# Where the mixer's result is transposed ahead of the out-projection in a two-layer decoder kernel

## The chip, the cores and the metric

The kernel runs on one core of one Trainium2 chip. The metric is the device time of one execution in microseconds; for several runs it is their median. A core has TensorE (PE in the profile; PEld is its weight load), VectorE (DVE), ScalarE (ACT), GpSimd (POOL) and SyncE (SP), which here only issues transfers.

## What is computed

Two layers over 256 tokens of width 1024, all in float32. Layer 0 mixes by retention and HGRN2, layer 1 by stick-breaking and differential attention; each has one combined input projection and one output projection. After each mixer stands a mixture of experts with 32 experts, of which each token uses two.

```python
for l in range(DEPTH):
    h = rms_norm(x, norm_mix[l])
    if l % 2 == 0:
        mix = retention_hgrn2_mixer(h, w_in_ab[j], w_out_ab[j], ...)
    else:
        mix = stickbreak_diff_mixer(h, w_in_cd[j], w_out_cd[j], ...)
    x = x + mix
    h = rms_norm(x, norm_ffn[l])
    x = x + hierarchical_moe(h, ..., w_gate[l], w_up[l], w_down[l])

# the end of either mixer; layer 0 as an example
    ret = rms_norm(ret, ret_gain).reshape(B, S, RET_WIDTH) * jax.nn.silu(rg)
    o = rms_norm(o, hgrn_gain).reshape(B, S, ...) * jax.nn.silu(hg)
    mixed = jnp.concatenate([ret, o], axis=-1)      # (1, 256, 1024)
    return mixed @ w_out                            # w_out: (1024, 1024)
```

## The kernel before

Every weight is used once and comes from HBM in units of 2048 KB. The SP queue issues them in one fixed order (`load_unit`, its transfer at L328) into eleven places: six in `ring`, five in `wide`. A place that was in use is waited for through the semaphore `unit_used`, which TensorE raises when it has done the last matmul on a unit. Per layer the order is: the blocks of the input projection (8 in layer 0, 6 in layer 1), the two halves of w_out (places 2 and 3), then 96 expert units. Expert units 0 to 3 use places 4, 5, 0, 1; then the queue waits until both halves of the mixer's result are gated (`gated`), issues units 4 to 7 into places 6 to 9 of `wide`, and units 8 and 9 into places 2 and 3, which the two halves of w_out must have left. Unit 10 waits for the router's logits (L796) and unit 11 for place 4, which the first expert matmuls free.

Each engine runs its own hand-written order of work. The part around the change:

- `project(layer, n)` multiplies the normalized tokens `hT` by block n (L741): 16 products of 128x128 by 128x512, each two records in the trace (x32), two token blocks (`tc`) of eight products. Results go to PSUM banks 0, 1 or 2, 3 in turn (`proj(g)`). Its argument `meanwhile` is a list of functions that are called after each quarter of the block. The last block of layer 0 is `project(0, 7)`, to banks 2 and 3. ACT takes its sigmoid (L1074), VectorE multiplies twice (L1409, and `gate_it` at L1424), and with that the second half of `mixed` is gated. The first half of `mixed` (retention) is gated by the same line one block earlier.
- `mixed` holds tokens on the partitions, so TensorE must transpose it before the out-projection: `turn_mixed(pe, half)` (L707), eight 128x128 transposes for each half into banks 0 and 1. The halves use the same banks. `keep_mixT` (L712) copies a turned half from PSUM to `hT`: the first half by ACT in `finish_mixer`, the second by VectorE in its own `finish_mixer`.
- `project_out(layer)` (L783) is, for each half: wait until it is gated, transpose it, wait for the copy, and do 16 products on it with that half of w_out, accumulating in banks 4 to 7, token block by token block. VectorE then adds to `x` (L1199).
- `route_and_experts` follows: x is transposed (L697, copied at L701), the router's logits are made (L796), VectorE selects (L1245 to L1292) and builds one-hot matrices (L596), TensorE gathers the tokens of four experts at a time (L475), and the expert matmuls run (L519) for eight quads of four experts. In quad 0 and in the last matrix the weights come in quarters over all four experts, and each quarter frees its unit by itself.
- In layer 1 the first half of `mixed` (stick-breaking) is gated by a copy at L1547 and the second at L1555, behind an inverse root that ACT and VectorE do together (`take_root`).
- `y_sb` is a buffer of 128x1024 that only the expert stage uses; it is cleared at L584 ahead of it.

Of the kernel before, what the change touches and what calls it, by code (L numbers as in the profile page):

```python
# [23 lines left out]
P = 128  # L24
SEQ = 256
# [100 lines left out]
def build(nc, t, where, const_width, stop_after=4):  # L126
    with ExitStack() as ctx:
        def sb(name, shape, dt=F32):
            return ctx.enter_context(nc.sbuf_tensor(name, shape, dt))

        def sem(name):
            return ctx.enter_context(nc.semaphore(name))
# [11 lines left out]
        psum = ctx.enter_context(nc.psum_tensor("psum", [P, 8, 512], F32))  # L144
# [4 lines left out]
        def part(who, width, shape=None, **dims):  # L149
            a = taken.get(who, 0)  # L150
            taken[who] = a + width
            assert taken[who] <= (arena_w, UNIT)[who == "last"], (who, taken)
            a += arena_w * (who == "last")
            v = wide[:, a:a + width]
            return v.rearrange(shape, **dims) if shape else v

        hT = part("last", KC * SEQ, "p (c t) -> p c t", c=KC)
# [48 lines left out]
        y_sb = sb("y_sb", [P, D])[:, :]  # L206
# [30 lines left out]
        S = {n: sem(n) for n in names}  # L237
        proj_used = [sem(f"proj_used{i}") for i in range(2)]
# [15 lines left out]
        def unit_base(layer):  # L254

            return layer * (UNITS_IN[0] + UNITS_OUT + n_moe)
# [28 lines left out]
        def slot(layer, n):  # L285

            place = unit_place(layer, n)
            return ring[:, place, :] if place < RING else wide[:, (place - RING) * UNIT:(place - RING + 1) * UNIT]
# [5 lines left out]
        def wait_unit(eng, layer, n):  # L294
            eng.wait_ge(unit_landed[unit_place(layer, n)], unit_landings(layer, n))
# [6 lines left out]
        def proj(g):  # L302

            return psum[:, 2 * (g % 2):2 * (g % 2) + 2, :]

        def wait_projected(eng, n):

            eng.wait_ge(S["unit_used"], n if n <= UNITS_IN[0] else unit_base(1) + n - UNITS_IN[0])

        def flat(a):  # L310
            return a.rearrange("p a b -> p (a b)")
# [336 lines left out]
        def take_root(act, turn):  # L648
            col, count = ROOTS[len(roots_taken)]
            roots_taken.append(col)  # L650
            act.wait_ge(S["root_in"], len(roots_taken))
            y = small[:, 64:64 + count]
            turn(nc.scalar.activation(y, small[:, col:col + count], ACT.Ln))
            nc.scalar.activation(y, y, ACT.Exp, scale=-0.5).then_inc(S["root_out"], 1)
# [48 lines left out]
        def turn_mixed(pe, half):  # L703

            for tc in range(TC):
                for c in range(4):
                    mm = pe.transpose(psum[:, c // 2, (c % 2) * SEQ + tc * P:(c % 2) * SEQ + (tc + 1) * P],  # L707
                                      mixed[:, tc, (4 * half + c) * P:(4 * half + c + 1) * P], ident)
            mm.then_inc(S["mix_turned"], 1)

        def keep_mixT(half, copy):
            return copy(hT[:, 4 * half:4 * half + 4, :].rearrange("p (b c) t -> p b (c t)", b=2), psum[:, 0:2, :])  # L712

        def keep_hT(half, copy):
            return copy(hT[:, 4 * half:4 * half + 4, :].rearrange("p (b c) t -> p b (c t)", b=2),  # L715
# [6 lines left out]
        def _(pe):  # L722
            def project(layer, n, meanwhile=()):


                g = (0, UNITS_IN[0])[layer] + n
                wait_unit(pe, layer, n)
                if g >= 2:

                    pe.wait_ge(proj_used[g % 2], g // 2)  # L730
                w = slot(layer, n).rearrange("p (c n) -> p c n", c=KC)
                banks = proj(g)
                if BLOCKS[layer][n] in TURNED[layer]:
                    for m in range(HEADS):
                        for c in range(KC):
                            mm = pe.matmul(banks[:, m // 2, (m % 2) * SEQ:(m % 2 + 1) * SEQ],  # L736
                                           w[:, c, m * P:(m + 1) * P], hT[:, c, :], start=c == 0, stop=c == KC - 1)
                else:
                    for tc in range(TC):
                        for c in range(KC):  # L740
                            mm = pe.matmul(banks[:, tc, :], hT[:, c, tc * P:(tc + 1) * P], w[:, c, :],  # L741
                                           start=c == 0, stop=c == KC - 1)
                            quarter = (tc * KC + c + 1) // (KC // 2)
                            if (c + 1) % (KC // 2) == 0 and quarter <= len(meanwhile):
                                meanwhile[quarter - 1]()
                mm.then_inc(S["unit_used"], 1)
# [6 lines left out]
            def attend(bank, hd, s, v):  # L753

                cols = slice(hd * HD, (hd + 1) * HD)
                pe.matmul(psum[:, bank, cols], s[:, 0:P], v[:, 0, cols], start=True, stop=True)
                pe.matmul(psum[:, bank + 1, cols], s[:, P:SEQ], v[:, 0, cols], start=True, stop=False)
                mm = pe.matmul(psum[:, bank + 1, cols], s[:, SEQ:TRI], v[:, 1, cols], start=False, stop=True)
                mm.then_inc(S["pv_done"], 1)

            def turn_roped(col):
# [4 lines left out]
                                          mixed[:, tc, col + hd * HD:col + (hd + 1) * HD], ident)  # L766
                mm.then_inc(S["turned"], 1)

            def project_out(layer):

                for half in range(2):

                    pe.wait_ge(S["gated"], 2 * layer + half + 1)
                    if half == 0:
                        pe.wait_ge(proj_used[0], (4, 7)[layer])
                    turn_mixed(pe, half)
                    pe.wait_ge(S["mixT_ready"], 2 * layer + half + 1)
                    wait_unit(pe, layer, UNITS_IN[layer] + half)
                    w = slot(layer, UNITS_IN[layer] + half).rearrange("p (c n) -> p c n", c=4)
                    for tc in range(TC):  # L780
                        for c in range(4):
                            for n in range(2):
                                mm = pe.matmul(psum[:, 4 + 2 * tc + n, :], hT[:, 4 * half + c, tc * P:(tc + 1) * P],  # L783
                                               w[:, c, 512 * n:512 * (n + 1)], start=half == 0 and c == 0,
                                               stop=half == 1 and c == 3)
                        if half == 1 and tc == 0:
                            mm.then_inc(S["out_first"], 1)
                    mm.then_inc(S["unit_used"], 1)
# [81 lines left out]
            pe.wait_ge(S["st_ready"], 2 * HEADS)  # L870
            for hd in range(HEADS):
                attend(4, hd, st2[:, hd, :], val2)
            project(0, 7)

            pe.wait_ge(S["out_used"], 2)
            project_out(0)
# [33 lines left out]
            def diff_turn(hd):  # L910

                pe.wait_ge(S["diff_a"], hd + 1)
                if hd >= 2:
                    pe.wait_ge(S["diff_aT"], hd - 1)
                a = dff[:, hd % 2, :]
                pe.transpose(psum[:, hd % 2, 0:P], a[:, 0:P], ident)
                pe.transpose(psum[:, hd % 2, P:SEQ], a[:, P:SEQ], ident)
                pe.transpose(psum[:, hd % 2, SEQ:TRI], a[:, SEQ:TRI], ident).then_inc(S["diff_turned"], 1)
# [30 lines left out]
            def diff_attend(hd):  # L949
                pe.wait_ge(S["diff_aT"], hd + 1)  # L950
                attend(2, hd, st[:, hd % 2, :], val2)
# [9 lines left out]
            for hd in range(2, HEADS):  # L961
                diff_turn(hd)
                diff_attend(hd)
            project_out(1)
            route_and_experts(1)

# [4 lines left out]
        def _(act):  # L971
# [14 lines left out]
                act.wait_ge(S["h_turned"], n // 2 + 1)  # L986
                keep_hT(0, nc.scalar.copy).then_inc(S["hT_ready"], 1)

            def finish_mixer(layer):

                act.wait_ge(S["mix_turned"], 2 * layer + 1)
                keep_mixT(0, nc.scalar.copy).then_inc(S["mixT_ready"], 1)
                nc.scalar.preload_act_table_set(LOG_EXP)
                square(act, 2 * layer + 1, 0)
                act.wait_ge(S["x_turned"], TC * layer + 1)
                keep_xT(0, nc.scalar.copy).then_inc(S["xT_first"], 1)
                square(act, 2 * layer + 1, 1)
                take_root(act, turn)
# [71 lines left out]
            act.wait_ge(S["pv_done"], 2 * HEADS)  # L1070
            nc.scalar.activation(tmp, flat(psum[:, 4:6, :]), ACT.Square).then_inc(S["sq_out"], 1)
            take_root(act, turn)
            wait_projected(act, 8)
            nc.scalar.activation(flat(qT), flat(proj(7)), ACT.Sigmoid).then_inc(S["gate_sig"], 1)  # L1074
            finish_mixer(0)
# [76 lines left out]
            act.wait_ge(S["pv_done"], 4 * HEADS)  # L1152
            nc.scalar.activation(tmp1, flat(psum[:, 2:4, :]), ACT.Square).then_inc(S["sq_out"], 1)
            take_root(act, turn)
            finish_mixer(1)
            route(1)
            moe_act(act, 1, 0, 0)
# [429 lines left out]
```

## Time and profile before

| what | value |
|---|---|
| median of 3 runs | 1288.95 us (1288.56 to 1290.48) |
| profiled execution | 1287.09 us |
| its span in the trace | 1285.1 us |
| PE busy | 993.1 us (77%) |
| VectorE busy | 243.0 us (19%) |
| ScalarE busy | 153.8 us (12%) |
| moved by DMA | 448.53 MB, mean 349 GB/s |
| L519, expert matmuls | 406.5 + 401.4 us |
| L741, in-projections, 128x512 | 145.5 us |
| L783, out-projections | 58.7 us |

The profile is one execution. Its own time is 2.0 us over its span. PE busy is no measure of load, since TensorE also shows as busy while it works at a lower clock; the granted clock stands in a row of its own. A chain of waits follows the execution back from its last instruction, at each step to what released it. Times are from the span's start; layer 0's mixer lasts to about 206 us, its experts to about 660, layer 1's mixer to about 826.

### The profile page before, as it was taken

Reading aid. Unit: us, or ns where it says so; the run is one execution under the profiler, and the core shown is the slowest. Engines: PE = TensorE matmul, PEld = TensorE weight load, DVE = VectorE, ACT = ScalarE, POOL = GpSimd, SP = SyncE. Lnnn points to the kernel's source line nnn. Section 1 sums busy time; section 2 is a strip of 40 time slices with the busy share of each in tenths; the row PEclk is TensorE's granted clock in tenths of the full one; section 3 lists DMA queues with packets and bytes.
Section 4 is the critical chain, followed back from the end, with each engine's and each line's share of the span. In section 5 each row is a group of like instructions: output and inputs, shape, how many; then the busy total and the mean of one; then the engine's idle time right before and its main releaser. Section 6 shows DMA issues by size and latency. Waiting matters only on the chain.

```text
span 1285.1 us, 12164 instructions
## 1 busy us (share of the span) xinstructions
PE 993.1 (77%) x5148; PEld 433.0 (34%) x5148; DVE 243.0 (19%) x668; ACT 153.8 (12%) x320; POOL 12.6 (1%) x12
## 2 busy tenths in 40 slices
PE   5999998986767776766759987997776867767765
PEld 5657645421212121212227544542212312121211
DVE  3410225111101000101030564331101101000101
ACT  3523311100000000000021222110000000000000
POOL 0000001000000000000000000100000000000000
PEclk9988899987879878878789998998877878778878
DMA  7963067899999999999997413869999999999995
GB/s 248 302 248 131 14 279 296 341 429 427 428 429 426 429 426 429 427 428 428 417 392 255 149 69 148 340 280 430 427 428 427 428 427 428 427 429 426 429 421 218
DMA packets 62150, 448.53 MB, mean 349 GB/s; under 512 B 13072, under 2 KB 13328, under 8 KB 39568
## 3 DMA queue, kind: packets, MB, share of 16 engines
q1 hardware_dynamic: 62096, 447.73, 84.5%
q8 instruction: 44, 0.72, 0.2%
q14 instruction: 10, 0.08, 0.0%
HBM read 446.66 MB, written 1.05 MB: 348 GB/s over the span
## 4 chain that ended last, share of the span: by engine, by line
DMA 48%; PE 42%; SPq 4%; DVE 3%; ACT 1%; issue 1%; DVEq 0%; ACTq 0%
PE psum L519 17%; DMA ring<-in_w_up 14%; PE psum L741 11%; DMA ring<-in_w_down 10%; DMA wide<-in_w_gate 10%; DMA wide<-in_w_down 9%; DMA ring<-in_w_gate 5%; PE psum L783 5%; PE psum L736 2%; SPq L384 2%; SPq L328 1%; PE psum L475 1%; PE psum L836 1%; PE psum L482 1%; PE psum L838 1%
## 5 line engine op out<-in xcount | busy, mean ns | idle before, releaser
L519 PE MATMUL psum<-ring,mixed 128*32 128x512 f32 x1664 | 406.5, 714 | 123.8 <-DMA ring<-in_w_up 54.2
L519 PE MATMUL psum<-wide,mixed 128*32 128x512 f32 x1408 | 401.4, 710 | 108.8 <-DMA wide<-in_w_gate 62.4
L519 PEld LDWEIGHTS psum<-ring,mixed 128*32 128x32 f32 x1664 | 93.0, 128 | 328.1 <-issue 162.0
L519 PEld LDWEIGHTS psum<-wide,mixed 128*32 128x32 f32 x1408 | 88.6, 127 | 274.1 <-issue 123.2
L741 PE MATMUL psum<-ring,wide 128*128 128x512 f32 x320 | 145.5, 613 | 0.6 <-DMA ring<-in_w_in_ab 0.6
L741 PEld LDWEIGHTS psum<-ring,wide 128*128 128x128 f32 x320 | 62.3, 198 | 76.9 <-issue 75.8
L623 DVE TENSOR_TENSOR mixed<-psum,sig 128x512 f32<-128x512 f32 x16 | 16.9, 1056 | 277.9 <-PE psum L519 277.9
L482 PE MATMUL psum<-y_sb,spread 128*128 128x512 f32 x144 | 66.6, 605 | 1.6 <-DVE y_sb L628 1.6
L475 PE MATMUL psum<-sel,h 128*128 128x128 f32 x520 | 64.4, 283 | 3.5 <-DVE sel L596 3.5
L475 PEld LDWEIGHTS psum<-sel,h 128*128 128x128 f32 x520 | 61.0, 196 | 17.1 <-issue 13.4
L783 PE MATMUL psum<-ring,wide 128*128 128x512 f32 x128 | 58.7, 618 | 6.1 <-ACT wide L712 3.5
L567 ACT COPY mixed<-psum 128x1024 f32<-128x1024 f32 x18 | 18.2, 1012 | 355.1 <-PE psum L475 355.1
L736 PE MATMUL psum<-wide,ring 128*128 128x256 f32 x256 | 57.3, 387 | 2.7 <-DVE wide L715 2.7
L620 DVE TENSOR_TENSOR sig<-psum,sig 128x512 f32<-128x512 f32 x16 | 11.1, 692 | 240.8 <-ACT sig L573 240.8
L736 PEld LDWEIGHTS psum<-wide,ring 128*128 128x128 f32 x256 | 49.5, 194 | 10.3 <-DVE wide L715 3.4
L628 DVE COPY y_sb<-psum 128x512 f32<-128x512 f32 x16 | 11.1, 692 | 194.0 <-PE psum L519 194.0
L604 DVE TENSOR_SCALAR selw<-consts,rank,wtab 128x32 f32<-128x32 f32 x144 | 31.4, 296 | 50.6 <-PE psum L548 50.5
L573 ACT ACTIVATE sig<-psum 128x512 f32<-128x512 f32 x16 | 9.6, 597 | 257.2 <-PE psum L519 257.2
L482 PEld LDWEIGHTS psum<-y_sb,spread 128*128 128x128 f32 x144 | 25.9, 189 | 42.7 <-issue 39.2
L783 PEld LDWEIGHTS psum<-ring,wide 128*128 128x128 f32 x128 | 25.0, 198 | 37.6 <-issue 30.4
L580 ACT COPY y_sb<-psum 128x512 f32<-128x512 f32 x16 | 9.4, 586 | 206.1 <-PE psum L519 206.1
L596 DVE TENSOR_SCALAR sel<-consts,rank,small 128x32 f32<-128x32 f32 x144 | 31.4, 295 | 1.6 <-PE psum L475 1.5
(238 smaller groups left out, 529.9 us busy)
## 6 DMA issues: line engine op xcount, KB each, us to landing
ring<-in_w_down SPq DMA_DIRECT2D x38, 2048.0 KB, 35.1
ring<-in_w_up SPq DMA_DIRECT2D x36, 2048.0 KB, 37.7
wide<-in_w_gate SPq DMA_DIRECT2D x34, 2048.0 KB, 36.6
ring<-in_w_gate SPq DMA_DIRECT2D x30, 2048.0 KB, 30.9
wide<-in_w_up SPq DMA_DIRECT2D x28, 2048.0 KB, 28.5
wide<-in_w_down SPq DMA_DIRECT2D x26, 2048.0 KB, 34.7
ring<-in_w_in_ab SPq DMA_DIRECT2D x8, 2048.0 KB, 16.6
ring<-in_w_in_cd SPq DMA_DIRECT2D x6, 2048.0 KB, 21.4
```

Of the source, the lines that this page charges most:

```text
L328: sp.dma_start(dst_cols(slot(layer, n)), src).then_inc(unit_landed[unit_place(layer, n)], 16)
L384: sp.dma_start(dst, src).then_inc(S["small_landed"], 16)
L475: mm = pe.matmul(psum[:, YB + c // 4, (c % 4) * P:(c % 4 + 1) * P], h[:, tc, c, :], sel[:, tc, :], start=tc == 0, stop=tc == TC - 1)
L482: mm = pe.matmul(psum[:, ACC + 2 * tc + n, :], spread[:, tc, :], y_sb[:, 512 * n:512 * (n + 1)], start=False, stop=False, skip_group_check ...
L519: mm = pe.matmul(psum[slots, out + n, :], inp[:, c, slots], slot(layer, unit)[:, at + 512 * n:at + 512 * (n + 1)], start=c == 0, stop=c == ...
L567: nc.scalar.copy(xT, psum[:, YB:YB + 2, :].rearrange("p b (c s) -> p (b c) s", s=P)).then_inc(m["xT_ready"], 1)
L596: r = nc.vector.tensor_scalar(sel[:, tc, e * SLOTS:(e + 1) * SLOTS], const("iota"), rank[:, tc, bass.ds(quad * TILE + e, 1)], small[:, 2 + ...
L604: r = nc.vector.tensor_scalar(selw[:, tc, e * SLOTS:(e + 1) * SLOTS], const("iota"), rank[:, tc, bass.ds(quad * TILE + e, 1)], wtab[:, tc, ...
L623: nc.vector.tensor_tensor(act_h.rearrange("p c s -> p s c"), psum[:, UP, :].rearrange("p (s c) -> p s c", c=FC), sig.rearrange("p (s c) -> ...
L736: mm = pe.matmul(banks[:, m // 2, (m % 2) * SEQ:(m % 2 + 1) * SEQ], w[:, c, m * P:(m + 1) * P], hT[:, c, :], start=c == 0, stop=c == KC - 1)
L741: mm = pe.matmul(banks[:, tc, :], hT[:, c, tc * P:(tc + 1) * P], w[:, c, :], start=c == 0, stop=c == KC - 1)
L783: mm = pe.matmul(psum[:, 4 + 2 * tc + n, :], hT[:, 4 * half + c, tc * P:(tc + 1) * P], w[:, c, 512 * n:512 * (n + 1)], start=half == 0 and ...
```

## The change

The second half of `mixed` is transposed into banks 2 and 3 in place of 0 and 1, and this is done in both layers between the first and the second token block of the first half's out-projection (`turn_half(layer, 1)`). The first half is transposed before `project_out`: in layer 0 inside the last in-projection, between its two token blocks, in layer 1 where it was. The first half's copy goes to `y_sb` in place of `hT`; on ACT it is a function of its own, `keep_first_half`, which stands in layer 0 ahead of the last gate's sigmoid. The waits for the gate and for the bank go with the transposes.

```diff
@@ -704,12 +704,16 @@
 
             for tc in range(TC):
                 for c in range(4):
-                    mm = pe.transpose(psum[:, c // 2, (c % 2) * SEQ + tc * P:(c % 2) * SEQ + (tc + 1) * P],
+                    mm = pe.transpose(psum[:, 2 * half + c // 2, (c % 2) * SEQ + tc * P:(c % 2) * SEQ + (tc + 1) * P],
                                       mixed[:, tc, (4 * half + c) * P:(4 * half + c + 1) * P], ident)
             mm.then_inc(S["mix_turned"], 1)
 
+        def mixT(half):
+
+            return hT[:, 4:8, :] if half else y_sb.rearrange("p (c t) -> p c t", c=4)
+
         def keep_mixT(half, copy):
-            return copy(hT[:, 4 * half:4 * half + 4, :].rearrange("p (b c) t -> p b (c t)", b=2), psum[:, 0:2, :])
+            return copy(mixT(half).rearrange("p (b c) t -> p b (c t)", b=2), psum[:, 2 * half:2 * half + 2, :])
 
         def keep_hT(half, copy):
             return copy(hT[:, 4 * half:4 * half + 4, :].rearrange("p (b c) t -> p b (c t)", b=2),
@@ -766,23 +770,26 @@
                                           mixed[:, tc, col + hd * HD:col + (hd + 1) * HD], ident)
                 mm.then_inc(S["turned"], 1)
 
+            def turn_half(layer, half):
+
+                pe.wait_ge(S["gated"], 2 * layer + half + 1)
+                pe.wait_ge(proj_used[half], (4, 7)[layer])
+                turn_mixed(pe, half)
+
             def project_out(layer):
 
                 for half in range(2):
-
-                    pe.wait_ge(S["gated"], 2 * layer + half + 1)
-                    if half == 0:
-                        pe.wait_ge(proj_used[0], (4, 7)[layer])
-                    turn_mixed(pe, half)
                     pe.wait_ge(S["mixT_ready"], 2 * layer + half + 1)
                     wait_unit(pe, layer, UNITS_IN[layer] + half)
                     w = slot(layer, UNITS_IN[layer] + half).rearrange("p (c n) -> p c n", c=4)
                     for tc in range(TC):
                         for c in range(4):
                             for n in range(2):
-                                mm = pe.matmul(psum[:, 4 + 2 * tc + n, :], hT[:, 4 * half + c, tc * P:(tc + 1) * P],
+                                mm = pe.matmul(psum[:, 4 + 2 * tc + n, :], mixT(half)[:, c, tc * P:(tc + 1) * P],
                                                w[:, c, 512 * n:512 * (n + 1)], start=half == 0 and c == 0,
                                                stop=half == 1 and c == 3)
+                        if half == 0 and tc == 0:
+                            turn_half(layer, 1)
                         if half == 1 and tc == 0:
                             mm.then_inc(S["out_first"], 1)
                     mm.then_inc(S["unit_used"], 1)
@@ -870,7 +877,7 @@
             pe.wait_ge(S["st_ready"], 2 * HEADS)
             for hd in range(HEADS):
                 attend(4, hd, st2[:, hd, :], val2)
-            project(0, 7)
+            project(0, 7, (lambda: None, lambda: turn_half(0, 0)))
 
             pe.wait_ge(S["out_used"], 2)
             project_out(0)
@@ -961,6 +968,7 @@
             for hd in range(2, HEADS):
                 diff_turn(hd)
                 diff_attend(hd)
+            turn_half(1, 0)
             project_out(1)
             route_and_experts(1)
 
@@ -986,10 +994,13 @@
                 act.wait_ge(S["h_turned"], n // 2 + 1)
                 keep_hT(0, nc.scalar.copy).then_inc(S["hT_ready"], 1)
 
-            def finish_mixer(layer):
+            def keep_first_half(layer):
 
                 act.wait_ge(S["mix_turned"], 2 * layer + 1)
                 keep_mixT(0, nc.scalar.copy).then_inc(S["mixT_ready"], 1)
+
+            def finish_mixer(layer):
+
                 nc.scalar.preload_act_table_set(LOG_EXP)
                 square(act, 2 * layer + 1, 0)
                 act.wait_ge(S["x_turned"], TC * layer + 1)
@@ -1070,6 +1081,7 @@
             act.wait_ge(S["pv_done"], 2 * HEADS)
             nc.scalar.activation(tmp, flat(psum[:, 4:6, :]), ACT.Square).then_inc(S["sq_out"], 1)
             take_root(act, turn)
+            keep_first_half(0)
             wait_projected(act, 8)
             nc.scalar.activation(flat(qT), flat(proj(7)), ACT.Sigmoid).then_inc(S["gate_sig"], 1)
             finish_mixer(0)
@@ -1152,6 +1164,7 @@
             act.wait_ge(S["pv_done"], 4 * HEADS)
             nc.scalar.activation(tmp1, flat(psum[:, 2:4, :]), ACT.Square).then_inc(S["sq_out"], 1)
             take_root(act, turn)
+            keep_first_half(1)
             finish_mixer(1)
             route(1)
             moe_act(act, 1, 0, 0)
```

## Rows read from the trace of the kernel before

**Rows 1.** The page, part 4: shares of the chain that ended last, by engine.

```profile
DMA 48%; PE 42%; SPq 4%; DVE 3%; ACT 1%; issue 1%; DVEq 0%; ACTq 0%
```

**Rows 2.** Stretches: length, busy time of five engines, granted clock, DMA share, GB/s.

```profile
217.00:221.00 4.00, 1.08 (x8) 0.97 (x8) 3.29 (x17) 1.49 (x2) 0.00 (x0) 1.00 0.44 188
221.00:225.00 4.00, 3.75 (x19) 3.75 (x20) 3.65 (x20) 0.00 (x0) 0.00 (x0) 0.57 0.00 0
840.00:845.00 5.00, 3.84 (x32) 3.65 (x32) 4.65 (x25) 0.69 (x1) 0.00 (x0) 1.00 0.00 0
...
231.00:620.00 389.00, 282.05 (x1700) 91.78 (x1692) 40.94 (x133) 20.72 (x35) 0.00 (x0) 0.84 1.01 427
849.00:1235.00 386.00, 278.19 (x1668) 90.81 (x1662) 40.85 (x133) 20.72 (x35) 0.00 (x0) 0.84 1.01 427
```

**Rows 3.** Timeline of the SP queue, issues of weight units: start, us, instruction.

```profile
177.80 1.76 SPq L328 DMA_DIRECT2D wide<-in_w_up  x4
...
229.81 0.33 SPq L328 DMA_DIRECT2D ring<-in_w_down  x1
231.53 3.76 SPq L328 DMA_DIRECT2D ring<-in_w_gate  x3
245.56 0.33 SPq L328 DMA_DIRECT2D wide<-in_w_gate  x1
...
847.39 0.33 SPq L328 DMA_DIRECT2D ring<-in_w_down  x1
```

**Rows 4.** Chain of waits, layer 0: start us, us, what.

```profile
160.39 13.75 PE psum L741 x32
174.16 1.02 ACT wide L1074
...
176.14 14.00 PE psum L783 x32
190.14 0.89 PE psum L707 x8
...
191.06 1.24 DVE wide L712
...
192.33 14.01 PE psum L783 x32
...
221.25 5.44 PE psum L475 x32
```

**Rows 5.** Chain of waits, layer 1.

```profile
792.64 16.68 PE psum L783 x32
809.32 0.89 PE psum L707 x8
810.23 1.24 DVE wide L712
811.51 14.02 PE psum L783 x32
...
840.43 3.84 PE psum L475 x32
```

**Rows 6.** Chain at 733.86 us; stretches there and before layer 1's out-projection.

```profile
733.86 0.87 PE psum L765 x8
...
733.00:735.00 2.00, 2.00 (x15) 1.71 (x15) 1.55 (x3) 1.10 (x2) 0.00 (x0) 1.00 0.77 174
...
788.00:798.00 10.00, 7.68 (x18) 4.18 (x18) 4.75 (x10) 3.62 (x5) 0.00 (x0) 0.50 0.19 52
```

**Rows 7.** Timeline of VectorE and ScalarE: gates of the halves, a table load.

```profile
160.13 1.22 DVE L1424 TENSOR_TENSOR mixed<-mixed,wide 128x1024 f32<-128x1024 f32 x1
...
163.41 1.28 ACT L1074 ACT_TABLE_LOAD   x1
...
176.55 1.23 DVE L1424 TENSOR_TENSOR mixed<-mixed,wide 128x1024 f32<-128x1024 f32 x1
...
793.99 1.29 DVE L1555 TENSOR_TENSOR mixed<-mixed,subln 128x512 f32<-128x512 f32 x2
```

## The prediction

> **What bounds the kernel now.** I read the chain of waits first. It is split almost evenly between waiting for DMA (48%) and TensorE work (42%) [rows 1]. A share over the whole span does not say which microseconds count, so the next question is where the DMA stream is unbroken. The table by stretch shows it: from 231 to 620 us and from 849 to 1235 us the DMA engines are busy all the time at 427 GB/s, while in 221 to 225 and in 840 to 845 us they move nothing [rows 2]. So each layer has two regimes: a mixer that TensorE and its waits pace, then an expert stage that the DMA paces. What ties them is the SP queue [rows 3]: after a gap an expert unit is issued at 229.81 in layer 0 and at 847.39 in layer 1, and the unbroken stream begins with it. Both issues wait for a ring place that the first expert matmuls (gate projection, quad 0) free. The stream then takes a fixed time, so an earlier start of the expert matmuls moves the end of the layer one for one. The chain through the mixer is therefore worth its full length.
>
> In that chain [rows 4], layer 0: last in-projection 160.39 to 174.16; ACT's sigmoid (1.02), then ACT's copy of the first turned half; first half of the out-projection 176.14 to 190.14; eight transposes (0.89); VectorE's copy of the second half (1.24); second half from 192.33. The first eight transposes lie beside the sigmoid. In layer 1 [rows 5]: 792.64 the first half, 809.32 transposes (0.89), 810.23 the copy (1.24), 811.51 the second half. While these copies run, TensorE has nothing.
>
> **The change part by part.**
>
> *Second half turned amid the first half's out-projection, both layers.* The eight transposes do not vanish: they stand after the first eight products of the half and cost 0.89 there as before. What goes is the wait for the copy: layer 0, 192.33 - (190.14 + 0.89) = 1.30; layer 1, 811.51 - (809.32 + 0.89) = 1.30 [rows 4, 5]. The copy now lies beside the remaining token block, half of 14.00 = 7.0 us, against its 1.24; that is the cover, 5.8 to spare. It can do so since the second half goes to banks 2 and 3, and the two halves' results no longer share banks.
>
> *First half turned amid the last in-projection, layer 0.* ACT copies it behind the sigmoid, from 174.16 + 1.02 = 175.18 to about 176.14 (so 0.96), and only then the out-projection starts [rows 4]. After the change the transposes stand near 160.39 + 13.75/2 = 167.3 and ACT copies to y_sb by about 169.2, with 5.8 us to spare. The in-projection ends later by the transposes. Their price bounded from both sides: 0.87 (eight transposes between two projections) [rows 6] and 0.89 [rows 4]; I take 0.88. The out-projection starts at 174.16 + 0.88 = 175.04 instead of 176.14: a gain of 1.10. In layer 1 the first half is turned and copied where it was, in the same order on ACT, so nothing is gained there.
>
> *Waits that are added or move.* Inside the in-projection TensorE now waits for the first half's gate. That gate, queued on VectorE, ends at 160.13 + 1.22 = 161.35 [rows 7], 5.9 us before TensorE comes by. Queued behind this wait is the second token block of the projection; it is not touched. Inside the out-projection TensorE waits for the second gate. In layer 0 this gate ends today at 176.55 + 1.23 = 177.78 [rows 7]; sigmoid and gate follow the end of the in-projection, so it moves to 178.66, and TensorE comes by at 175.04 + 7.0 = 182.04: 3.4 to spare. In layer 1 it ends at 793.99 + 1.29 = 795.28 [rows 7], and TensorE comes by about 7.0 before 809.32, at 802.3. ACT's copy now stands ahead of the sigmoid in ACT's queue; the sigmoid's table load (1.28) [rows 7] may slip behind the copy, to about 170.5, still ahead of 175.04. None costs anything while these margins hold; if the second gate were 4 us later, TensorE would wait for the rest.
>
> *The SP queue.* It waits for the second gate too, so in layer 0 its four units at 177.80 go out 0.88 later. A unit of 2048 KB takes about 4.9 us at 427 GB/s, and the unit before it is freed by the in-projection's end, at 175.04; so the engines still have work until about 180. The unit that the first half of w_out frees goes out with the end of that half, today 176.14 + 14.00 = 190.14, then 175.04 + 14.00 + 0.88 = 189.92; the two behind it, for the second half and the logits, about 2.4 earlier. After the restart four units are on the way (229.81 and three from 231.53), 19.7 us of transfer, and the next release comes at 245.56, 15.8 after 229.81 [rows 3]: the stream has no hole, and these releases move with TensorE.
>
> *Sum.* Layer 0: 1.10 + 1.30 = 2.40. Layer 1: 1.30. Together 3.70. The profiled execution took 1287.09 us (span 1285.1 and 2.0 around it): 1287.09 - 3.70 = 1283.4. The median of the runs is 1288.95, so by the same sum **1285.2 us**.
>
> *What the trace leaves uncertain: the clock.* The 32 gather matmuls took 5.44 in layer 0 [rows 4] and 3.84 in layer 1 [rows 5]; in the first the granted clock was at 1.2 GHz for part of the time (0.57 on the mean in 221 to 225), in the second at 2.4 GHz (1.00 in 840 to 845) [rows 2]. Ahead of the slow one TensorE was busy for 1.08 of 4 us, in 217 to 221 [rows 2]. So the chain of a layer varies by 1.60 with where the fall lies, and a shift of the work by 2.4 us can move it either way: both gathers slow, or both fast. This gives 1285.2 + 1.6 = 1286.8 and 1285.2 - 1.6 = 1283.6. The Trainium skill (TensorE: Matmul & The Clock Gate, What's actually happening) says that the same kernel shows a differing number of slow matmuls from run to run, since the monitor is not aligned with its start; no single trace can show that.
>
> **The rivals.** By 0.2% (2.6 us) I mean about what a measurement of this kernel can tell from no change.
>
> *Rival 1, the clock draw takes the gain:* both gathers in the slow clock, 1286.8, 0.17% faster and so no measurable change. For it: one of two did so before. Against: equally likely the other way.
>
> *Rival 2, the stream holds the end:* the DMA share of 48% is what counts, and an earlier mixer only lengthens a wait. 1288.95. Against it: nothing moves in 221 to 225, and the releases at 229.81 and 847.39 are TensorE's.
>
> *Rival 3, the early turn in layer 0 does not do what it says:* the wait inside the in-projection or ACT's queue gives back the 1.10, and the layer 0 copy gives only part: 1.3 to 2.6 in all, 1286.9 at 2.1. Against: margins of 3.4 to 5.9.
>
> *Rival 4, slower:* transposes amid matmuls pull the clock down. A low stretch of TensorE with small work ahead of it cost much in layer 1: 788 to 798 ran at 0.50 [rows 6], and that out-projection half took 16.68 [rows 5] where its twin took 14.00 [rows 4], 2.68 more. If each of the three insertion places brought one such stretch: 3 x 2.68 - 3.70 = +4.3, 1293.3. It decides from two such stretches on (5.4 against 3.7); over 0.2% needs three. Against: eight transposes between two projections stand at 733.86, and the clock in 733 to 735 is 1.00 [rows 6], with dense matmuls on both sides, just as in the new places. The Trainium skill (TensorE: Matmul & The Clock Gate, Part 4: PE-mode transpose) states the rule behind this rival: transposes do not count as busy like matmuls do, and the full clock does not engage for them. By that rule short insertions might lower the clock; the trace disagrees at the one place that resembles the new ones.
>
> **How the numbers follow.** Forecast, 1285.2 with the gathers mixed as before: 0.60, faster. Both gathers fast, 1283.6: 0.11, faster. Rival 1: 0.14, the same. Rival 2: 0.06, the same. Rival 3: 0.05, the same. Rival 4: 0.04, slower. In the runs of before the highest lies 1.5 over the median; a repeated median of either kernel may move by about 1, which adds little on the slower side beyond rival 4. Faster 0.71, same 0.25, slower 0.04. The range takes in 1283.6 less 0.8 and 1286.8 plus 1.5: 1282.8 to 1288.3; rival 4 and most of rival 2 are left out.
>
> **What would show it.** In the changed kernel's chain: the copies at the two turns are gone from it, and each second half of the out-projection follows the first within 0.1 us; the first half in layer 0 starts within 0.1 of the in-projection's end; both halves with transposes last 14.9 (17.6 in layer 1 if the clock is again low). The copy of the first half on ACT stands near 168 to 169. The restart of the SP queue moves from 229.81 to about 227.4, give or take 1.6 with the clock, and that of layer 1 comes 3.7 earlier. The prediction is wrong if TensorE shows a wait for a gate inside either projection, if the clock is 0.50 behind an insertion, or if the time from restart to end grows.

## The result and the profile after

The changed kernel took 1282.45 us (median of 5 runs, 1280.83 to 1283.33), the kernel before 1288.95 (5 runs, 1288.35 to 1290.48). The ratio is 0.9946, with a 95% interval of 0.9931 to 0.9960: faster by 6.5 us, where 3.7 were forecast, and the time lies 0.35 below the range. All runs of both kernels together, told below, put the gain at 4.5 us. So there are two things to explain, 0.8 us that the sum lacked and 2 us that the first comparison showed too much.

The page of the changed kernel; its shares cannot be told from those of before [rows 1]:

```profile
span 1280.5 us, 12166 instructions
...
PE 993.7 (78%) x5148; PEld 434.5 (34%) x5148; DVE 243.0 (19%) x668; ACT 153.9 (12%) x320; POOL 12.6 (1%) x12
...
DMA 48%; PE 42%; SPq 4%; DVE 3%; ACT 1%; issue 1%; DVEq 0%; ACTq 0%
```

The chain of waits in layer 0 (start us, us, what), the answer to [rows 4]:

```profile
160.19 6.87 PE psum L745 x16
167.06 0.87 PE psum L707 x8
167.93 6.87 PE psum L745 x16
174.80 6.87 PE psum L788 x16
181.67 0.87 PE psum L707 x8
182.54 20.62 PE psum L788 x48
...
218.06 3.84 PE psum L475 x32
```

Line 745 is the in-projection, 707 the transposes, 788 the out-projection. The chain no longer leaves TensorE between 160.19 and 203.16. From the start of the last in-projection to VectorE's add of the second token block it is 203.18 - 160.19 = 42.99; before it was 206.37 - 160.39 = 45.98, the add's start being 192.33 + 14.01 and an issue of 0.03 behind it [rows 4]. That is 2.99 saved, where the sum had 2.40. The transposes cost 0.87 at both places, as forecast. The half with its transposes takes 6.87 + 0.87 + 6.87 = 14.61, and not the 14.9 that I wrote.

Layer 1, the answer to [rows 5]:

```profile
788.10 9.95 PE psum L788 x16
798.05 0.87 PE psum L707 x8
798.92 20.62 PE psum L788 x48
...
834.44 5.46 PE psum L475 x32
```

The SP queue (issues of weight units), the answer to [rows 3]:

```profile
178.47 1.76 SPq L328 DMA_DIRECT2D wide<-in_w_up  x4
...
225.02 0.33 SPq L328 DMA_DIRECT2D ring<-in_w_down  x1
...
843.03 0.33 SPq L328 DMA_DIRECT2D ring<-in_w_down  x1
```

The restart of the stream moved from 229.81 to 225.02 in layer 0, 4.8 earlier and 0.8 below the forecast's lower bound (227.4 - 1.6 = 225.8). 3.2 of it are the mixer's (0.2 of them lie before the last in-projection), and 1.6 are the gather: it took 3.84 here against 5.44 [rows 4]. In layer 1 it is the other way round, 5.46 against 3.84 [rows 5]. So the clock's part cancels in this pair of profiles. The expert stages keep their pace, 428 GB/s below against 427 [rows 2]. The two profiled executions, 1287.09 and 1282.45, thus differ by 4.6 us, and not by 6.5: 3.2 in layer 0's mixer and 1.45 in layer 1's, where the way from the start of the out-projection to the add went from 825.55 - 792.64 = 32.91 [rows 5] to 819.56 - 788.10 = 31.46. The slow records at its start are not at the same clock in the two; at an equal clock layer 1 is compared below.

The covers and margins of the prediction, on the timelines of ScalarE and VectorE:

```profile
167.97 1.01 ACT L716 COPY y_sb<-psum 128x1024 f32<-128x1024 f32 x1 [4.78 <-PE psum L707]
169.00 1.28 ACT L1086 ACT_TABLE_LOAD   x1
...
177.22 1.23 DVE L1437 TENSOR_TENSOR mixed<-mixed,wide 128x1024 f32<-128x1024 f32 x1
182.58 1.22 DVE L716 COPY wide<-psum 128x1024 f32<-128x1024 f32 x1 [4.13 <-PE psum L707]
```

The first half's copy stands at 167.97 (forecast 168 to 169), and the table load did slip behind it, to 169.00, done 4.5 us before the in-projection ends and the sigmoid can start. The second gate ends at 178.45 and TensorE comes by at 181.67, 3.2 later (forecast 3.4). The second copy, 182.58 to 183.80, lies beside matmuls until 189.4.

Stretches (length, busy time of five engines, granted clock, DMA share, GB/s) around the two insertions of layer 0 and of the stream:

```profile
160.00:174.00 14.00, 14.00 (x41) 6.75 (x40) 5.67 (x9) 3.73 (x5) 0.00 (x0) 1.00 0.32 130
174.00:190.00 16.00, 16.00 (x44) 7.48 (x43) 3.67 (x3) 2.31 (x2) 0.00 (x0) 1.00 0.90 363
...
230.00:620.00 390.00, 283.76 (x1676) 93.49 (x1673) 41.65 (x134) 21.32 (x36) 0.00 (x0) 0.83 1.01 428
```

The granted clock is 1.00, that is 2.4 GHz, across both insertions; the third, in layer 1, has 1.00 as well (798 to 799).

### The profile page after: what moved, and what is told of

The parts are those of the page before. It is cut to its first block, busy times and chain, and to the rows that moved or that the text cites. A ratio compares the mean times of both kernels' runs of the same rounds, so it can differ in the third digit from the quotient of the medians.

```text
span 1280.5 us, 12166 instructions
## 1 busy us (share of the span) xinstructions
PE 993.7 (78%) x5148; PEld 434.5 (34%) x5148; DVE 243.0 (19%) x668; ACT 153.9 (12%) x320; POOL 12.6 (1%) x12
## 4 chain that ended last, share of the span: by engine, by line
DMA 48%; PE 42%; SPq 4%; DVE 3%; ACT 1%; issue 1%; DVEq 0%; ACTq 0%
PE psum L519 17%; DMA ring<-in_w_up 14%; PE psum L745 11%; DMA ring<-in_w_down 10%; DMA wide<-in_w_gate 10%; DMA wide<-in_w_down 9%; DMA ring<-in_w_gate 5%; PE psum L788 5%; PE psum L740 2%; SPq L384 2%; SPq L328 1%; PE psum L475 1%; PE psum L843 1%; PE psum L482 1%; PE psum L845 1%
## 5 line engine op out<-in xcount | busy, mean ns | idle before, releaser
L519 PE MATMUL psum<-ring,mixed 128*32 128x512 f32 x1664 | 411.8, 722 | 124.4 <-DMA ring<-in_w_up 52.1
L745 PE MATMUL psum<-ring,wide 128*128 128x512 f32 x320 | 145.5, 612 | 1.9 <-DMA ring<-in_w_in_ab 1.9
L745 PEld LDWEIGHTS psum<-ring,wide 128*128 128x128 f32 x320 | 62.2, 198 | 77.5 <-issue 75.2
L788 PE MATMUL psum<-ring,y_sb 128*128 128x512 f32 x64 | 31.0, 642 | 2.3 <-ACT y_sb L716 2.3
L788 PE MATMUL psum<-ring,wide 128*128 128x512 f32 x64 | 27.8, 592 | 0.0
```

Source lines behind the costliest of these rows:

```text
L519: mm = pe.matmul(psum[slots, out + n, :], inp[:, c, slots], slot(layer, unit)[:, at + 512 * n:at + 512 * (n + 1)], start=c == 0, stop=c == ...
L788: mm = pe.matmul(psum[:, 4 + 2 * tc + n, :], mixT(half)[:, c, tc * P:(tc + 1) * P], w[:, c, 512 * n:512 * (n + 1)], start=half == 0 and c ...
```

## Experiments

The theories, made after the result above was seen. **A**: the change is worth the waits that it removes, 3.7 us, and at each of the three also a restart of TensorE, 0.26 us (work behind a wait takes that much longer than the same work behind running work), which the sum lacked; 4.5 in all, and the rest of the 6.5 is scatter. **B**: the waits had a further cost; in part of the executions the clock fell in them, which made a slow tail in the kernel before. **C**, the rival from the prediction, that the DMA stream holds the end, was tried at a larger size as well.

### The parts alone, and both kernels again

The kernel before, unchanged:

> The kernel before, unchanged, once more. Theory A (the profiled execution of before was a lucky draw, and the change is worth its removed waits plus a TensorE restart of 0.26 us each): ratio 1.000, times between 1287 and 1291 as before, and its trace has no low clock at the two copies of the turned halves (174 to 176 and 190 to 193 us). Theory B (the idle ends at these copies let the clock fall in part of the executions of before, and this is the rest of the gain): a trace of before shows a granted clock below 1.00 in 176 to 206 us, and more time there.

Measured: 1287.66 us median, ratio 1.0006 (0.9991 to 1.0020). The kernel before beside it, 35 runs on the same chip, had a median of 1287.48, a mean of 1288.0 and a range of 1284.98 to 1292.44. So the three runs of the prediction, median 1288.95, lay high, and one run scatters by more than 2 us. In its trace the clock is 1.00 all the way from 160 to 206, and the halves of the out-projection take 14.00 and 14.02: no fall at the copies, as theory A expected.

The whole change:

> The whole change, once more. Theory A: 3.7 us of removed waits plus three restarts of 0.26 us, so 4.5 us faster, ratio 0.9965. Theory B: 6.5 us faster, ratio 0.995.

Measured: 1283.56 us, ratio 0.9967 (0.9956 to 0.9978), theory A's number. Theory B's 0.995 lies outside the interval.

The second half alone:

> Only the second half is turned amid the first half's out-projection, in both layers; the first half of layer 0 is turned behind the in-projection as before. Theory A: two waits of 1.30 and two restarts of 0.26, so 3.1 us faster, ratio 0.9976. Theory B: more than that, about 4.5, since two idle stretches are gone.

```diff
-            project(0, 7, (lambda: None, lambda: turn_half(0, 0)))
+            project(0, 7)
+            turn_half(0, 0)
...
-            keep_first_half(0)
             wait_projected(act, 8)
             nc.scalar.activation(flat(qT), flat(proj(7)), ACT.Sigmoid).then_inc(S["gate_sig"], 1)
+            keep_first_half(0)
```

Measured: 1284.55 us, ratio 0.9966 (0.9950 to 0.9982). That is theory B's number (4.5 us), though the interval holds theory A's 0.9976 too. The stretch of the trace is sharper and speaks for A: layer 0 from the last in-projection's start to the add takes 203.37 - 158.96 = 44.41, 1.57 less than the 45.98 of before, against 1.56 by theory A.

The first half alone:

> Only the first half of layer 0 is turned amid the last in-projection; the second halves are turned between the two halves of the out-projection as before, though into banks 2 and 3. Theory A: 1.10 and one restart of 0.26, so 1.4 us faster, ratio 0.9989. Theory B: about 2, ratio 0.9984.

```diff
                 for half in range(2):
+                    if half == 1:
+                        turn_half(layer, 1)
                     pe.wait_ge(S["mixT_ready"], 2 * layer + half + 1)
...
-                        if half == 0 and tc == 0:
-                            turn_half(layer, 1)
```

Measured: 1286.45 us, ratio 0.9984 (0.9973 to 0.9995), which does not tell the theories apart. The same stretch of its trace takes 205.67 - 161.09 = 44.58, 1.40 less than before; theory A said 1.36. Its chain shows the restart itself, since here one half of the out-projection follows the in-projection at once and the other follows a copy:

```profile
175.70 13.73 PE psum L790 x32
189.44 0.89 PE psum L707 x8
190.35 1.24 DVE wide L716
191.63 14.02 PE psum L790 x32
```

The same 32 records take 13.73 in the first case and 14.02 in the second. The transposes behind an unbroken stream, followed by a wait, are billed 0.89, not 0.87. A stop costs its wait and also some 0.26 to 0.29 us. What TensorE does in them no row shows; I call it the restart.

### The waits filled, the wait put back

If the clock fell in the waits of the kernel before, keeping TensorE busy in them should help:

> The kernel before with two extra matmuls (128x128 by 128x256 of the constant tables, results unused) on TensorE while it waits for a copy: behind the turn of the first half in layer 0 and behind the turn of the second half in both layers. The waits stay, TensorE is not idle in them. Theory A (only the removed waits and the restarts count, and the slow tail of before, 10 of 35 executions over 1290 us, has nothing to do with these places): median as before within 0.5 us, same tail over 1290. Theory B (in part of the executions the clock falls in these waits, which makes the tail, and none of 17 executions of the changed kernel has one): the tail is gone, the mean 0.5 to 1 us lower.

```diff
+            def fill(bank, n):
+                for _ in range(n):
+                    pe.matmul(psum[:, bank, 0:SEQ], ident, ones, start=True, stop=True, skip_group_check=True)
...
                     turn_mixed(pe, half)
+                    if half == 1:
+                        fill(2, 2)
+                    elif layer == 0:
+                        fill(4, 2)
```

Measured: 1287.96 us median, 1284.98 to 1293.41, ratio 1.0003 (0.9985 to 1.0020); 4 of 12 executions lie over 1290. The tail is still there, and the mean, 1288.7, is not lower. The profiled execution was one of the tail, 1290.58 us, and it too has the clock at 1.00 from 160 to 206 and the halves at 14.00 and 14.02. Theory B falls. The chain shows where this execution lost time:

```profile
221.42 3.84 PE psum L475 x32
...
651.26 3.37 PE psum L519 x16
...
673.73 30.00 PE psum L736 x128
...
794.74 17.04 PE psum L791 x32
...
1272.36 3.43 PE psum L519 x16
```

The same places in the repeated kernel before, which took 1287.31:

```profile
221.41 5.47 PE psum L475 x32
...
652.86 1.97 PE psum L519 x16
...
673.78 27.91 PE psum L736 x128
...
792.96 16.72 PE psum L783 x32
...
1270.48 1.97 PE psum L519 x16
```

The last 16 expert records of a layer (line 519), behind the last wait for weights, take 1.97 in one and 3.37 and 3.43 in the other; the gather (line 475) takes 5.47 in one and 3.84 in the other. These are the same instructions at the two levels of the clock: its mean over the last 16 is 0.58 and 0.57 in the slow case and 1.00 in the other. The out-projection of layer 1 (line 783, 791 with the added lines) is slow in both, a little more in the first. The first 128 in-projection records of layer 1 (line 736) take 30.00 and 27.91. All these rows together make 3.6 us, and the two executions differ by 3.3. Slow last records of layer 0 come with slow first in-projection records: 3.31 to 3.37 with 29.97 to 30.00 in four traces (this one, the changed kernel's second and third repeat, and the one with a delay in the mixers, all below), 1.97 with 27.91 in the other ten, so this one draw is worth 3.4 us. All of it but the out-projection lies outside of what the change touches.

The wait for the second copy, put back into the changed kernel:

> The changed kernel, but TensorE waits for the copy of the second half directly behind its transposes, ahead of the second token block of the first half. This gives back the wait for the copy in both layers and nothing else. Theory A: 2 x (1.30 + 0.26) = 3.1 us slower than the changed kernel, 1.4 us faster than before, ratio 0.9989; the restart shows as 0.26 us on the matmuls behind the wait. Theory B: in addition some executions with a slow tail, over 1289 us.

```diff
                         if half == 0 and tc == 0:
                             turn_half(layer, 1)
+                            pe.wait_ge(S["mixT_ready"], 2 * layer + 2)
```

Measured: 1286.45 us, 1282.91 to 1288.42, ratio 0.9982 (0.9966 to 0.9998). Expected was 0.9989. The changed kernel beside it:

> The changed kernel a third time, beside the others. Theory A: 4.5 us faster than before (ratio 0.9965), 3.1 faster than the kernel with the wait put back. Theory B: 5.5 to 6.5 us faster on the mean, since before has the tail and this has not.

Measured: 1284.76 us, 1279.57 to 1286.71, ratio 0.9975 (0.9960 to 0.9990), a gain of 3.6 us by the means where theory A has 4.5. The difference of the two, 1.7 by the medians and 1.9 by the means, is short of 3.1, but each mean of 12 runs has a standard error of 0.5 to 0.6, so the times neither confirm 3.1 nor rule it out. In the traces the clock can be held equal. In layer 1 the first 16 records took 9.75 both here and in the kernel with the second half alone. With the wait:

```profile
793.41 9.75 PE psum L788 x16
803.16 0.89 PE psum L707 x8
804.08 1.24 DVE wide L716
805.36 20.88 PE psum L788 x48
826.26 1.23 DVE x L1213
```

Without it:

```profile
790.35 9.75 PE psum L788 x16
800.09 0.87 PE psum L707 x8
800.97 20.62 PE psum L788 x48
821.61 1.23 DVE x L1213
```

826.26 - 793.41 = 32.85 against 821.61 - 790.35 = 31.26, a difference of 1.59 where theory A has 1.56. In layer 0 the stretch is 205.92 - 161.35 = 44.57 with the wait and 42.99 without, 1.58.

### A known delay in either stage

> The changed kernel with 20 unused matmuls (128x128 by 128x256, 0.43 us each at full clock, 8.6 us together) on TensorE ahead of the out-projection of each layer. If the mixer's chain passes one for one to the end: 8.6 in layer 0, in layer 1 8.6 less the 2.3 in which TensorE waits there anyway, 6.3; together 14.9 us slower than the changed kernel, ratio to before about 1.008. If the DMA stream holds the end, well under half of it.

```diff
+            fill(4, 20)
             project_out(0)
...
             turn_half(1, 0)
+            fill(4, 20)
             project_out(1)
```

> The changed kernel with the same 20 unused matmuls in the expert stage instead, ahead of the third matrix of quad 3 in each layer, where TensorE waits some 31 us per quad for weights. If the stream sets the end from its restart on: 0 us, ratio to before as the changed kernel, 0.9965. If TensorE's work counts there: 17 us slower.

```diff
                 pe.wait_ge(m["xT_ready"], n17 + i + 2)
+                if not over and i == 3:
+                    for _ in range(20):
+                        pe.matmul(psum[:, YB, 0:SEQ], ident, ones, start=True, stop=True, skip_group_check=True)
                 matrix(i, 2, YB, actT, FC, D)
```

In the mixers: 1297.70 us, ratio 1.0069 (1.0048 to 1.0091), mean of 5 runs 1297.4, against the changed kernel's 1283.6 (below) 13.8 us, uncertain by 2 to 3. In the expert stage: 1283.70, ratio 0.9972 (0.9955 to 0.9989), mean of 10 runs 1283.9, 0.3 us. The same work costs most of its length in one stage and nothing that can be seen in the other. The chain with the delay in the mixers:

```profile
174.81 8.63 PE psum L781 x40
...
799.87 9.51 PE psum L781 x40
809.38 6.87 PE psum L792 x16
```

In layer 1 the filling (line 781) takes the low clock upon itself, 9.51 instead of 8.63, and the 16 out-projection records behind it run in 6.87 instead of 9.95. From the last attention records to the end of these 16 it is 816.24 - 797.26 = 18.98 here and 798.05 - 782.95 = 15.10 in the changed kernel. So layer 1 costs 3.9 (6.3 expected), and both layers 12.5 where 14.9 were expected; the measured 13.8 decides for neither. (The profiled execution itself, 1300.09, has both gathers at 5.47 and the last expert records of layer 0 at 3.31.) With the delay in the experts:

```profile
405.36 8.90 PE psum L554 x40
414.26 7.01 PE psum L519 x64
421.28 28.31 DMA ring<-in_w_up
```

The 8.90 us of filling (line 554) stand in front of a wait for weights. It begins later than in the changed kernel, 421.28 against 418.96, and ends where that one ends, 449.59 against 449.70. The stream did not change. The other traces say the same of the whole stage: from the first expert matmul to the start of the last 16 records it takes 424.4 to 425.0 us in layer 0 and 424.3 to 424.8 in layer 1 in all 14 traces, whether layer 0's begins at 221.3, as in the second repeat of the changed kernel, or at 234.4, as with the delay in the mixers. So rival 2 of the prediction is refuted, and what it was made of, a stream that cannot be hurried, is right for the other stage.

### Filling the waits where the clock does fall

> The changed kernel with unused matmuls (128x128 by 128x256) in TensorE's waits at other places: 3 and 4 of them while the router selects, in both layers, and 11 between the last attention steps of layer 1 and its out-projection. If the low clock comes from these idle stretches: both gathers at 3.8 us in place of one at 5.4, and the first 16 out-projection records of layer 1 at 7.1 in place of 9.8; 1.6 + 2.7 = 4.3 us faster than the changed kernel, and less scatter. If the clock falls all the same, the same time as the changed kernel within 1 us.

```diff
                 start_sums(pe, layer, 0)
+                fill(7, 3)
...
+                fill(7, 4)
                 moe_pe(pe, layer, 0, 0)
...
                 diff_turn(hd)
+                fill(6, 1)
                 diff_attend(hd)
+                if hd == 2:
+                    fill(6, 3)
             turn_half(1, 0)
+            fill(6, 6)
```

> The changed kernel with the 11 unused matmuls between the last attention steps of layer 1 and its out-projection alone, none in the router. The first 16 out-projection records of layer 1 at 7.1 us in place of 9.8 in each execution: 2.7 us faster than the changed kernel on the mean. If what is won there is lost later to another fall of the clock, less.

```diff
                 diff_turn(hd)
+                fill(6, 1)
                 diff_attend(hd)
+                if hd == 2:
+                    fill(6, 3)
             turn_half(1, 0)
+            fill(6, 6)
```

> The changed kernel once more, beside the others. Theory A (removed waits 3.7 plus three restarts of 0.26): 4.5 us faster than before on the mean of many executions. Theory B (a further systematic gain from the clock): 5.5 or more.

Measured, all places filled: 1283.48 us, 1278.10 to 1287.48, ratio 0.9971 (0.9955 to 0.9987), no gain over the changed kernel to be seen. Only the places ahead of the out-projection of layer 1: **1280.37 us**, 6 runs from 1279.45 to 1282.16, ratio 0.9945 (0.9926 to 0.9963). The changed kernel beside it: 1284.94, ratio 0.9965 (0.9948 to 0.9981). The version with 11 unused matmuls is the fastest of all; its mean of six, 1280.5, is 3.1 us under the changed kernel's 1283.6 (uncertain by about 1). Its chain and a stretch of its clock, then the chain of the changed kernel beside it, and the same stretch of the clock in the changed kernel's first trace, whose out-projection starts at the same 788.10:

```profile
788.10 7.13 PE psum L792 x16
...
782.00:797.00 15.00, 14.25 (x58) 8.84 (x59) 5.61 (x11) 4.10 (x6) 0.00 (x0) 1.00 0.36 134
```

```profile
790.84 10.15 PE psum L788 x16
...
782.00:797.00 15.00, 12.06 (x31) 6.34 (x30) 4.75 (x10) 4.11 (x6) 0.00 (x0) 0.66 0.37 137
```

16 records in 7.13 instead of 10.15 (9.83 to 10.16 in the changed kernel's four traces), with the clock at 1.00 instead of 0.66 on the mean. The gain of the mean is about what this one line is shorter by, 2.7 to 3.0. That it comes from there is shown for the line and not for the time: with all places filled the line is as short, 7.13, and the mean is no lower.

That all places together gave nothing is explained in part. In its trace both gathers are fast (3.76), but the filling in the router's wait is itself on the chain in front of one:

```profile
218.39 1.81 PE psum L781 x8
220.20 3.76 PE psum L475 x32
```

From the add of x to the first expert matmul it is 225.11 - 204.17 = 20.94 there and 223.04 - 203.18 = 19.86 in the changed kernel with an equally fast gather: 1.1 us lost in layer 0. In layer 1 it is 19.87, nothing lost, and 1.6 less than in the changed kernel, whose gather there is slow. Its last 16 expert records of layer 1 were slow (3.37). The profiled execution took 1280.66; why the mean of the twelve is 1283.6 one trace can't tell, and it stays open.

## Why the prediction was wrong

**The direction, the places and the mechanism were right.** The three waits are gone, the transposes keep their price (0.87), the margins are within 0.3 us of the forecast, the restart of the stream passes a microsecond on as a microsecond (the known delay), and the SP queue's later second gate cost nothing.

**The step that failed in the sum is the price of a removed wait.** I took the gap between two rows, 1.10, 1.30 and 1.30. A stop of TensorE costs also its restart: 0.59 more in layer 0 for two stops (2.99 against 2.40) and 0.29 more in layer 1 for one (1.59 against 1.30). The rows were there: 32 records took 13.75 behind running work and 14.00, 14.01 and 14.02 behind a wait [rows 4, 5], and I used the 14.00 as the length of the work. With 3 x 0.26 the sum is 4.5. The same slip made the two halves with their transposes 14.9 long in the forecast, where 14.61 were measured.

**The second thing that was off is the starting value.** I took the median of three runs for the time before. The runs of all comparisons together:

| kernel | runs | mean | standard deviation | range |
|---|---|---|---|---|
| before | 111 | 1288.08 | 2.20 | 1284.00 to 1294.53 |
| changed | 41 | 1283.60 | 2.12 | 1279.07 to 1287.14 |

The difference is 4.48 us, uncertain by 0.8 (95%), and theory A had 4.48. These runs include the ten of the first comparison, which raised the question; without them it is 4.24, uncertain by as much. The median that I started from was 0.9 above the mean of before, and the first median of the changed kernel, 1282.45, lies 1.15 below its mean. So the 6.5 are 3.7 of the sum, 0.8 of restarts, 0.9 and 1.15 of scatter, and the last two are luck. They were no small luck: the first comparison's interval, 0.9931 to 0.9960, leaves theory A's 0.9965 out, and its means differ by 7.0, about two standard errors above 4.24. The width below the forecast, 2.4, was not too small. With a standard deviation of 2.2 a median of three has a standard error of about 1.5 and one of five of 1.2, together 1.9, and 8 in 10 is 2.4 either way. Around 1285.2 that ends at 1282.8 and just misses; with the restarts in the sum, or from the mean 1288.1, it would have been centred on 1284.4 and reached 1282.0, so either of the two would have held the time. That the excess of the first comparison is nothing but scatter is inferred from the runs together; no trace of those executions of before exists, apart from the profiled one, which at 1287.09 lay below the rest.

**The clock rivals.** Rival 1 was right in that the shift moves the gathers' clock: slow in layer 0 and fast in layer 1 in both traces of before, fast and slow in all four of the changed kernel. In these traces it follows the kernel and not the execution, and it took nothing, since one is slow either way. Both slow, which the rival priced, is there with the second half alone and with the delay in the mixers. It was wrong in taking them for the only such place. The runs show more: the last 16 expert records of each layer, 1.97 or about 3.4; the start of layer 1's out-projection, 9.75 to 10.16 for 16 records where nothing fills the wait; and the first 128 in-projection records of layer 1, 27.91 or 30.00. The last in-projection of layer 0, too, begins anywhere between 158.44 and 161.35, for which I have no row. Rival 4, transposes that pull the clock down, is refuted: 1.00 across all three insertions. The Trainium skill's rule (TensorE: Matmul & The Clock Gate, Part 4: PE-mode transpose) that transposes do not hold the clock up is not contradicted by that; it is shown that eight of them between dense matmuls do no harm. Rival 3 did not happen.

## What to carry to other kernels

A wait of TensorE in the chain costs its gap and its restart: compare how long the same work takes behind running work and behind a stop, and take the shorter one as its length (here 13.73 against 14.00 to 14.02). Ask from the profile which stage sets when the transfers start again; only there is a microsecond a microsecond, and the same 8.6 us cost nothing one stage later. For a change of 0.3%, compare stretches of traces at equal clock: in all four traces of the changed kernel the stretch in layer 0 took 42.99, where its medians of 12 runs lay 1.4 us apart.

## What the runs showed of the hardware

- The restart: 0.26 to 0.29 us for 32 records of 128x512 behind a wait (14.00 to 14.02 against 13.73 to 13.75). The Trainium skill (TensorE: Matmul & The Clock Gate, Single matmul latency) gives a single bf16 matmul at full clock a constant of 398 cycles on top of its columns. As an estimate from that page, if a stop costs this constant once, it is 0.17 us, less than measured here in float32.
- The clock: the same 16 records of a layer's last expert matmuls took 1.97 or 3.31 to 3.43 us from one execution to the next, with the same wait for weights ahead of them (24.09 to 24.13 us in the changed kernel's four traces). The Trainium skill (same page, What's actually happening) says that the number of slow matmuls differs from run to run of one kernel, and the traces agree.
- Unused matmuls of 128x256 in TensorE's waits, 11 of them, kept the clock at 1.00 over a stretch (782 to 797) where it otherwise had a mean of 0.66, and the 16 records behind them took 7.13 instead of 9.83 to 10.16. The kernel with these alone was 3.1 us faster on the mean of six runs. In the router's wait, in front of the gather, such matmuls cost 1.1 us in layer 0 and nothing in layer 1.
